# Hybrid HGRN2/MLA block: six steps of the mixer placed earlier, and two head pairs' queries transposed by VectorE and DMA instead of TensorE

## What is computed

```python
h = rms_norm(x, attn_norm_w)
hq, hf, hi, hg, c_q, c_kv, k_r = split(h @ w_in)      # 4 x 1024, 512, 512, 64 columns
o_a = hgrn2_mixer(hq, hf, hi, hg, ...)                # gated linear recurrence, 8 heads, chunks of 64
q = (rms_norm(c_q) @ w_uq)    # 8 heads x 192; the last 64 get the rotary turn
k, v = from (rms_norm(c_kv) @ w_ukv) and k_r          # 8 heads
o_b = softmax(q k^T * scale, block-causal mask) @ v
x = x + concat([o_a, o_b]) @ w_out
gate, up = split(rms_norm(x) @ w_gate_up)             # 2 x 5632
x = x + (silu(gate) * up) @ w_down
```

## Time and profile before

| | |
|---|---|
| median of 3 runs | 1129.92 us (1129.71 to 1131.63) |
| the profiled execution | 1129.12 us, span 1127.4 us |
| granted TensorE clock, mean | 0.998 |
| TensorE matmuls busy | 1112.1 us, 99% |
| VectorE busy | 894.0 us, 79% |
| ScalarE busy | 642.0 us, 57% |
| Pool busy | 64.8 us, 6% |
| mean DMA rate | 208 GB/s |

### The profile page before, as it was taken

How to read it: one execution, slowest core, us unless ns; L and a number is a source line. 1 busy time by engine, 2 the same in 40 slices (tenths; PEclk the granted TensorE clock), 3 DMA queues, 4 the chain that set the end, 5 groups by cost and what they waited for, 6 DMA issues and landing times.

```text
span 1127.4 us, 15411 instructions
## 1 busy us (share of the span) xinstructions
PE 1112.1 (99%) x5225; PEld 935.8 (83%) x5225; DVE 894.0 (79%) x1217; ACT 642.0 (57%) x909; POOL 64.8 (6%) x159
## 2 busy tenths in 40 slices
PE   8999999999999999999999999999999999999998
PEld 7978888887888888888888888888888888888887
DVE  5679786588776567688888988988988879889777
ACT  7557866567764556454554554554554555555553
POOL 3010000010000000000010010010000010000000
PEclk9999999999999999999999999999999999999999
DMA  8687455556554455667677677677677786666665
GB/s 266 190 268 223 147 153 167 156 175 206 179 193 167 155 184 180 192 215 233 225 232 235 222 233 238 219 232 240 217 238 225 231 273 220 208 206 195 209 194 168
DMA packets 108919, 234.23 MB, mean 208 GB/s; under 512 B 8601, under 2 KB 19650, under 8 KB 108610
## 3 DMA queue, kind: packets, MB, share of 16 engines
q1 hardware_dynamic: 101346, 209.30, 58.0%
q0 software_dynamic: 7216, 24.12, 7.3%
q10 hardware_dynamic: 304, 0.14, 0.0%
HBM read 220.94 MB, written 12.58 MB: 207 GB/s over the span
## 4 chain that ended last, share of the span: by engine, by line
PE 90%; DVE 5%; ACT 2%; DMA 1%; issue 1%; POOL 0%; DVEq 0%; ACTq 0%; POOLq 0%; SPq 0%
PE side L1984 24%; PE main L1766 19%; PE side L1986 12%; PE main L1769 9%; PE side L1956 4%; PE side L1958 4%; PE side L1957 4%; PE main L1958 3%; PE main L1957 3%; PE main L1956 3%; DMA raw<-in_w_in 1%; DVE w_lo L1134 1%; PE side L1882 1%; PE side L1789 1%; ACT w_hi L793 1%
## 5 line engine op out<-in xcount | busy, mean ns | idle before, releaser
L1027 ACT CAST w_hi<-raw 128x1024 fp32r<-128x1024 f32 (+1 forms) x245 | 241.6, 990 | 173.0 <-PE side L1984 102.4
L1605 DVE TENSOR_TENSOR w_lo<-raw,w_hi 128x1024 fp32r<-128x1024 f32 (+1 forms) x245 | 275.5, 1139 | 22.3 <-ACT w_hi L1027 22.0
L1134 DVE TENSOR_TENSOR w_lo<-raw,w_hi 128x1024 fp32r<-128x1024 f32 (+3 forms) x156 | 178.4, 1153 | 105.5 <-ACT w_hi L793 103.4
L793 ACT CAST w_hi<-raw 128x1024 fp32r<-128x1024 f32 (+3 forms) x156 | 153.7, 993 | 139.8 <-PE main L1766 131.2
L1766 PE MATMUL main<-w_hi,hT_hi 128*128 128x512 f32 (+2 forms) x448 | 173.3, 388 | 2.1 <-DVE hT_lo L1155 0.9
L1769 PE MATMUL main<-w_hi,hT_lo 128*128 128x512 f32 (+2 forms) x448 | 169.1, 378 | 0.0
L1984 PE MATMUL side<-w_hi,hT_hi 128*128 128x512 f32 x400 | 155.6, 389 | 0.0
L1986 PE MATMUL side<-w_hi,hT_lo 128*128 128x512 f32 x400 | 155.6, 389 | 0.0
L1766 PE MATMUL main<-w_lo,hT_hi 128*128 128x512 f32 (+2 forms) x448 | 114.8, 378 | 0.0
L1984 PE MATMUL side<-w_lo,hT_hi 128*128 128x512 f32 x400 | 106.9, 389 | 0.0
L1766 PEld LDWEIGHTS main<-w_hi,hT_hi 128*128 128x128 f32 x448 | 84.8, 189 | 15.9 <-DVE hT_lo L1155 1.9
(11 more groups left out here) (293 smaller groups left out, 1836.0 us busy)
## 6 DMA issues: line engine op xcount, KB each, us to landing
raw<-in_w_gate_up SPq DMA_DIRECT2D x176, 512.0 KB, 4.8
raw<-in_w_down SPq DMA_DIRECT2D x88, 512.0 KB, 4.4
raw<-in_w_in SPq DMA_DIRECT2D x64, 512.0 KB, 4.4
raw<-in_w_out SPq DMA_DIRECT2D x32, 512.0 KB, 3.7
raw<-in_w_in SPq DMA_DIRECT2D x15, 384.0 KB, 4.4
squares<-hiddenT POOLq DMA_DIRECT2D x11, 512.0 KB, 5.2
hiddenT<-squares POOLq DMA_DIRECT2D x44, 128.0 KB, 4.9
raw<-in_w_ukv SPq DMA_DIRECT2D x8, 512.0 KB, 3.7
```

The costliest lines, as they stand in the source:

```text
L793: copy(w_hi[:, slot, 0:n], raw[:, slot, 0:n]).then_inc(s_hi, 1)
L1027: copy(w_hi[:, n % RING, 0:cols], src).then_inc(s_hi, 1)
L1134: tt(w_lo[:, slot, 0:n], raw[:, slot, 0:n], w_hi[:, slot, 0:n].bitcast(F32), ALU.subtract)\
L1605: tt(w_lo[:, n % RING, 0:cols], src, w_hi[:, n % RING, 0:cols].bitcast(F32), ALU.subtract)\
```

## The change

Three groups of steps get earlier positions in `schedule()`: `lat_t` 0 moves from granules 30 and 31 to 28 and 29 (`lat_t` 1 stays at 36 and 37); `scan` moves two granules earlier (48 to 46, 95 to 93) and `lev_a` of level 1 one (48 to 47, 95 to 94); `o_a` 0 moves from 80 to 77, `o_b` 0 and its `swap` from 81 to 78. The queries of head pairs 0 and 1 are no longer transposed by TensorE: VectorE transposes 32x32 blocks of `stage` and `stage_r` (512 and 256 elements a partition) into a new tile `heads` at granules 36 and 56, Pool moves it out and in, between hq0's swap and the load of bounds, and ScalarE copies it into `qTn` and `qTr` at granules 44 and 66 (before: `q_t` at 39 and 59). The four side uses of these `q_t` are gone, and `scores` waits on a new semaphore.

```diff
-        s += [(e + 13 - 2 * i + n, ("lat_t", i, n)) for n in range(2)]
+        s += [(e + 11 + n, ("lat_t", i, n)) for n in range(2)]
...
-        s += [(q - early, ("q_a", j)), (q - 1 if early else q + 1, ("q_b", j)), (q + 4, ("q_t", j))]
+        s += [(q - early, ("q_a", j)), (q - 1 if early else q + 1, ("q_b", j))]
+        s += [(q + 1, ("swap", "q", j)), (q + 9 + 2 * j, ("q_t", j))] if j < MOVED_HEADS else [(q + 4, ("q_t", j))]
...
-        s += [(p, ("scan", g))]
+        s += [(p - 2, ("scan", g))]
         for l in range(1, LEVELS + 1):
-            s += [(p, ("lev_a", g, l)), (p + 1, ("lev_b", g, l)), (p + 4, ("pairs", g, l))]
+            s += [(p - (l == 1), ("lev_a", g, l)), (p + 1, ("lev_b", g, l)), (p + 4, ("pairs", g, l))]
...
-        p = max(p + 10, END[("hg", g)] + 2, END[("ukv", 2)] + 3)
+        p = max(p + 10, END[("hg", g)] + 2, END[("ukv", 2)])
...
-    if kind in ("q_t", "k_t"):
+    if kind == "k_t" or kind == "q_t" and step[1] >= MOVED_HEADS:
         return [(step + (0,), "act"), (step + (1,), "act")]
...
+        heads = mb("heads", [P, P // Q, NT * 2 * Q + NT * Q])
...
+            for j in range(MOVED_HEADS):
+                swap("q", j)
             pool.wait_ge(s_lbused, 1)
...
+                    if kind == "q_t" and j < MOVED_HEADS:
+                        key = ("q", j)
+                        landed(*key)
+                        straight = swap_of[key][:, :, 0:2 * NT * Q].rearrange("p a (t h r) -> p t h a r", t=NT, r=Q)
+                        turned = swap_of[key][:, :, 2 * NT * Q:].rearrange("p a (t r) -> p t a r", r=Q)
+                        for h in range(2):
+                            copy(by_quarter(plain[:, 2 * j + h, :]), straight[:, :, h, :, :])
+                        for h in range(2):
+                            part = slice(h * ROPE, (h + 1) * ROPE)
+                            ins = copy(by_quarter(qTr[part, j % 2, h, :]), turned[part, :, :, :])
+                        ins.then_inc(s_heads, 1)
+                        return
...
+                    elif what == "q":
+                        dve.wait_ge(s_stage, 2 * i + 1)
+                        if i:
+                            dve.wait_ge(s_heads, i)
+                        straight, turned = [swap_of[a][:, :, c0:c1].rearrange("p b (n r) -> p n b r", r=Q)
+                                            for c0, c1 in ((0, 2 * NT * Q), (2 * NT * Q, 3 * NT * Q))]
+                        nc.vector.transpose(straight, stage[:, 0, :, :, 0:NOPE].rearrange("p t h (b c) -> p (t h) b c", c=Q))
+                        nc.vector.transpose(turned, stage_r[:, 0, :, :, :].rearrange("p t h (b c) -> p (t h) b c", c=Q))\
+                            .then_inc(s_swap, 1)
...
-                elif kind in ("q_t", "k_t"):
+                elif kind == "k_t" or kind == "q_t" and a[0] >= MOVED_HEADS:
...
                     given(("k_t", h // 2, 1))
+                    if h // 2 < MOVED_HEADS:
+                        pe.wait_ge(s_heads, h // 2 + 1)
```

More of the change, by code:

```diff
@@ L51 @@
 LEVELS = 5
+MOVED_HEADS = 2
 RING = 4
@@ L454, in hybrid_layer @@
         swap_of = {("lat", 0): hbT[:, :, :], ("lat", 1): hkT[:, :, :], ("o", 0): hgate.rearrange("p t (a c) -> p (t a) c", a=2)}
+        for j in range(MOVED_HEADS):
+            swap_of[("q", j)] = heads[:, :, :]
         swap_of[("hq", 0)] = E[:, 0, :].rearrange("p (a c) -> p a c", a=P // Q)
@@ L534, in hybrid_layer @@
         s_landed = sem("s_landed")
+        s_heads = sem("s_heads")
         s_turned = sem("s_turned")
@@ L722, in swap @@
                 n, at = SWAP[key], swap_of[key]
+                wide = at.shape[2]
                 pool.wait_ge(s_swap, n + 1)
-                pool.dma_start(swapped[n].rearrange("a c b x -> (a c) b x"), at).then_inc(s_parked, 16)
+                pool.dma_start(swapped[n, :, :, :, 0:wide].rearrange("a c b x -> (a c) b x"), at).then_inc(s_parked, 16)
                 pool.wait_ge(s_parked, 16 * (n + 1))
                 for b in range(P // Q):
-                    pool.dma_start(at[Q * b:Q * (b + 1), :, :], swapped[n, :, :, b, :].rearrange("a c x -> c a x"))\
+                    pool.dma_start(at[Q * b:Q * (b + 1), :, :], swapped[n, :, :, b, 0:wide].rearrange("a c x -> c a x"))\
                         .then_inc(s_landed, 16)
@@ L1270, in step @@
                         swap(a, latents[i][:, :, :])
+                    elif what == "q":
[5 more added lines that the diff above has]
+                        nc.vector.transpose(straight, stage[:, 0, :, :, 0:NOPE].rearrange("p t h (b c) -> p (t h) b c", c=Q))
+                        nc.vector.transpose(turned, stage_r[:, 0, :, :, :].rearrange("p t h (b c) -> p t (h b) c", c=Q))\
+                            .then_inc(s_swap, 1)
                     elif what == "hq":
@@ L1313, in step @@
                     reciprocal((kind[0] + "_a",) + a, inv[:, 0:4], 4)
-                    if j:
+                    if kind == "q_b" and 0 < j <= MOVED_HEADS:
+                        dve.wait_ge(s_swap, SWAP[("q", j - 1)] + 1)
+                    elif j:
                         dve.wait_ge(s_side, USE[(kind[0] + "_t", j - 1, 1)] + 1)
```

## The result

The changed kernel takes 1135.3 us (median of 6 runs, 1134.0 to 1136.49), the kernel before beside it 1129.51 us (6 runs, 1128.63 to 1131.63). The ratio is 1.005, with a 95% interval of 1.0039 to 1.006: slower by 5.8 us. The forecast was 1133.9 us, 4.0 us slower, in a range of 1127.0 to 1136.5. The profiled execution of the changed kernel took 1136.38 us with a span of 1134.0 us, so the two spans differ by 6.6 us. Half a microsecond of that (0.55) is there before the first step that the change moves, in the waits for `hT_lo` of the start-up; the change accounts for the other 6.05 us.

The account below looks back on a forecast made before the run. TensorE was taken as the bound, busy 1112.1 of 1127.4 us. Terms 0.3 + 2.6 - 1.5 - 0.4 - 0.7 + 2.0 + 1.7 = +4.0 us gave 1133.9 us, range 1127.0 to 1136.5.

Parts of the forecast that it names:

- Latent splits, then pair 0's transposes: First stretch, to granule 44: splits earlier -1.3; pair 0's transposes -0.7 on TensorE, +2.3 of waits; together +0.3 us.
- Pool's queue: Pair 0's queries through DRAM: the DMAs aren't late, and the loads and swap behind them are wanted only later; no cost.
- Where ScalarE picks them up: ScalarE's copies of pair 0's queries at granule 44, in its full stretch: `scores` 0 waits for the keys' copy, +2.6 us.
- Scans: Earlier `scan` and `lev_a`: `pairs` 1 and `probs_t` 1 no longer wait, -1.5 us; in the second group -0.4 us.
- Pair 1: Head pair 1's six transposes gone from TensorE: -0.7 us, the extra VectorE and ScalarE work hidden.
- the cover: Granules 56 to 66, where ScalarE waits for TensorE, hide pair 1's extra work; without that it would cost 1.5 us.
- First output: `o_a` at granule 77: `q_t` 2 waits 5.4 us for its bank, old waits of 3.4 us go, +2.0 us.
- The clock: Lower clock level behind the 5.4 us gap at `q_t` 2, charged once: +1.7 us (0 to 2.5).
- rival (c): The clock falls twice, also behind the 2.6 us wait of `scores` 0: +5.7 us, 1135.6 us, chance 0.13.
- Rival (a): `q_t` 2's bank wait doesn't form, as ScalarE and VectorE reach `o_b` some 5 us sooner: -3.1, 1126.8 us, chance 0.17.
- (b): `q_t` 2's bank wait comes without the clock's fall: +2.3 us, 1132.2 us, chance 0.15.
- (d): Everything added is hidden, all gaps and moved transposes go: -11.2 us, 1118.7 us, chance 0.05.

Follow-up runs that it names:

- tuned kernel: Kernel before with 21 steps moved by an order fitted to head pair 1's queries via DRAM, pair 0's by TensorE: 1121.56 us, ratio 0.9934.

## Why the prediction was right in sign and short in size

- **Latent splits, then pair 0's transposes** (+0.3): measured +0.1. Each of the first waits came where it was put: 1.1, 0.3, 1.1 and 1.3 us, against 1.3, 0.6, 1.3 and 1.6. But only the sum holds, not my split into -1.3 and +1.6. Alone, the latent splits are at +0.75 by granule 44 and the queries at -0.65: what makes VectorE late here is the first move, and where pair 0 stays on TensorE the price of that move is `q_t` 0's wait of 1.7 us for `stage_r`, as two runs show. VectorE has the two transposes at 0.71 and 0.40 us, ahead of `w_lo` 40:

```profile
103.17 0.71 DVE L1298 STREAM_TRANSPOSE heads<-stage 128x512 f32<-128x512 f32 x1
103.81 0.40 DVE L1299 STREAM_TRANSPOSE heads<-stage_r 128x256 f32<-128x256 f32 x1
104.13 1.18 DVE L1155 TENSOR_TENSOR w_lo<-raw,w_hi 128x1024 fp32r<-128x1024 f32 x1
```

- **Pool's queue** (nothing): right. The tile goes out at 104.50 and its four loads are issued from 108.61 to 110.80, 11 us before ScalarE's copies at 122.15; neither pair's copies wait for `landed`:

```profile
104.50 0.72 POOL L731 DMA_DIRECT2D swapped<-heads  x1 [2.12 <-DVE heads L1299]
...
108.61 2.19 POOL L734 DMA_DIRECT2D heads<-swapped  x4 [3.38 <-DMA swapped<-heads]
```

- **Where ScalarE picks them up** (+2.6): the wait is 2.29 us by its row and 2.4 from start to start (my own terms, 137.1 less 134.6, give 2.5). The copies were cheaper than I took them, 0.6 us for the two straight ones instead of 0.95, but still in the range from 0.6 to 1.1 us. Leaving them out moved the wait by 1.6 us.
- **Scans** (-1.5, -0.4): -1.4 at `pairs` 1 and -0.2 at `probs_t` 1, then -0.4; -1.7 alone by the medians. **Pair 1** (-0.7): -0.7, all at granule 59 where `q_t` 1 stood; the cover held.
- **First output** (+5.4 -3.4): 5.50 us by the row, 5.7 from start to start, and -3.25. ScalarE's and VectorE's rows are at the places of the forecast, but all 2.8 us later (2.3 for what went before, and 0.5 of the start-up), where the prediction had this chain standing still: k_b2's root after the same 3.60 us wait as in the earlier trace rows, `o_b` on VectorE at 244.86 for 2.16 us.

```profile
236.46 0.21 ACT L835 ACTIVATE stat<-stat 128x4 f32<-128x4 f32 x1 [3.60 <-DVE stat L1190]
...
244.86 2.16 DVE L1502 SCALAR_TENSOR_TENSOR E<-side,stat,hgate 128x128 f32<-128x128 f32 x8
```

- **The clock** (+1.7): this is the mis-sized term. I charged one fall, behind the 5.4 us gap, at the price of the old one. There were two. The one behind `scores` 0's wait cost 1.7 us (4.1 for granules 49 to 51, less 2.4 of wait from start to start). The one behind `q_t` 2's cost 2.4 (5.40 us for work of 2.98), since the level stayed low for 6.8 us, 1.7 of them in the gap itself. Together 4.1 instead of 1.7, so 2.4 more than charged. The table's two sums differ by 2.05, since small terms nearly cancel: +0.3 for the longer bank wait, +0.35 between granules 44 and 49 (0.1 with the four copies left out, 0 with all queries by TensorE, so it comes with the copies), +0.1 at 82 to 89; against them -0.65 at 76 to 82 (`o_a` takes 2.60 us at its new place and took 3.06), -0.2 in the first stretch, -0.2 at `scores` 0's wait. The two falls are the rule in this kernel: five of its six executions have the mean clock of the profiled one, 0.995, one has 0.997. That was rival (c), at 1135.6; the time measured is 1135.3. That these agree within 0.3 us is in part luck, since (c) priced the second fall 0.7 too low and the small terms made up for it. I had the row for it: the 2.65 us gap of the earlier trace rows brought a fall, and I forecast a gap of 2.6. I should have charged it there and kept "one fall" as the rival.
- Rival (a), that the bank wait doesn't form, fell with the row of 5.50 us: the upstream stalls moved ScalarE and TensorE together (both 2.8 us). (b) fell with the clock of 0.50. (d) fell at the first new wait.

The two rules of the Trainium skill, against these runs. With pair 1's transposes off TensorE the tuned kernel is at 0.9934, with them on it at 0.9942, intervals overlapping; with pair 0's off it too it is at 0.9961, so pair 0's are better on it. By "VectorE: DVE Perf Modes", section Rules for kernel authors, 128x128 transposes belong on TensorE where a PSUM result will do; pair 0's ratios agree, pair 1's don't contradict it by more than the intervals. The rule has no condition; "whenever VectorE is full" in the prediction was mine, and the engine whose full stretch decided was ScalarE. "TensorE: Matmul & The Clock Gate", section Why this matters for your kernels, warns of long idle gaps between bursts; the trace agrees behind the gap of 5.5 us. The gaps of 2.0 to 2.65 us with a clock of 0.50 behind them are shorter than those that its table warns of, and there the measurement decides.

## What to carry to other kernels

Before a step that fills a shared bank is moved earlier, list who asks for that bank next in the rotation and when the slowest reader of it is done: the move here cost 5.5 us and a clock fall with the next user at granule 79, and no wait in the tuned order with it at 81 and the hq1 swap out of the reader's way. When work is taken off the bounding engine, the price is read where it is picked up: 1.45 us of copies in a full stretch of ScalarE cost 2.5 us by the medians and 3.2 by the profiles, and up to there the transposes on VectorE and the DMAs had cost next to nothing. And a forecast gap as long as one that has a clock fall behind it in the same trace should be charged with a fall of its own.

## What the runs showed of the hardware that I had not expected

The length of a gap alone doesn't say whether the clock falls. Behind single waits of 1.1 to 1.8 us it stayed at 1.00 in every trace here; behind 2.01, 2.2, 2.3, 2.65 and 5.5 us in the mixer it was at 0.50 for 3.4 or 6.8 us. But the tuned order with all queries by TensorE has a wait of 2.06 us at 89.58 with the clock at 1.00 all around it, while the kernel with both pairs via DRAM fell behind 2.01 us. And at the start-up, once the clock is up, the tuned kernel with pair 1 via DRAM waits 2.54 us and has no fall behind it; the queries alone have 2.29 us there, with none either:

```profile
89.58 0.47 PE L1790 MATMUL main<-w_hi,hT_hi 128*128 128x512 f32 x1 [2.06 <-issue]
...
88.00:96.00 8.00, 6.42 (x28) 5.35 (x29) 6.50 (x14) 7.69 (x18) 0.56 (x1) 1.00 0.63 194
```

```profile
16.43 0.44 PE L1820 MATMUL main<-w_hi,hT_hi 128*128 128x384 f32 x1 [2.54 <-DVE hT_lo L1200]
...
14.00:24.00 10.00, 7.57 (x47) 7.48 (x48) 8.21 (x15) 9.34 (x21) 0.85 (x1) 1.00 0.91 271
```

And two gaps of 0.99 and 1.87 us close together brought 6.8 us at the lower level. The same 5.5 us wait was followed by 3.4 us of it in one kernel and by 6.8 us in three. One kernel isn't constant in this either: of the 21 executions of the kernel before beside the second group of runs, five have a mean clock of 1.0 and spans of 1126.5 to 1127.3 us (median 1126.9), ten have 0.998 and spans of 1127.0 to 1128.3 (median 1127.55). Of the 11 with the first output back at its old place, four have 1.0 (median 1128.5) and five 0.998 (median 1130.2). So a fall behind a gap of 2.0 to 2.65 us is a chance and not a rule, and when it comes it is worth 0.65 us of the whole time in the one kernel and 1.7 in the other, though the rows price both at 1.7. What decides it, and where the rest of the price goes in the first kernel, these runs don't show.
